# Second layer of a four-layer block: convolution steps split up, z in a buffer of its own, scans and gates on other slots

## The chip, the cores and the metric

One NeuronCore of a Trainium2 chip runs the whole program. The metric is the device time of one execution in microseconds (us), the median of three runs. The engines are TensorE (PE; PEld is its weight load), VectorE (DVE), ScalarE (ACT), GpSimd (POOL) and SyncE (SP), which issues most of the DMAs.

## The reference, cut to what matters

Four layers work on an activation of 256 rows by 2048 columns, in float32. Each layer is: RMS norm, one wide input projection, mixers, a gate, an output projection. The change touches the second one (`odd_layer`):

```python
proj = rmsnorm(x, norm_g) @ w_in
xc, zc, qd, kd, vd, zd, a_pre, b_pre = split_cols(proj, OD_SIZES)
xconv = causal_dwconv(xc, conv_c_w) + conv_c_b              # 4 taps
yc = rg_lru(xconv, gate_w, gate_b, lam) * silu(zc)          # a scan along the 256 rows
qkv = silu(causal_dwconv(concat([qd, kd, vd]), conv_d_w))   # 4 taps
q, k, v = split(qkv, 3); q = l2norm(q); k = l2norm(k)
od = gated_delta_chunkwise(q, k, v, beta, g)
yd = rmsnorm(od, onorm_g) * silu(zd)
y = concat([yc, yd]) @ w_out
```

The kernel does the delta rule over two blocks of 128 rows for each head. The inverse of the unit triangular matrix is made from 16x16 blocks on DVE and then by doubling on PE (levels 4, 5 and 6).

## The kernel before, in words

**Pieces.** All weights come as 626 pieces of at most 128x1024 in float32. ACT copies a piece into a rounded high part (WH, L1062, the function `split`), DVE subtracts for the low part (WL, L1427), and PE multiplies three products of high and low parts (L711 to L713 where rows are the output's partitions, L735 to L737 where features are). Eight raw buffers (L629 loads them), six WH and eight WL buffers are used in turn. During piece p, ACT and DVE split piece p+5.

**Jobs.** Eight pieces (four for some) make a job of 512 output columns, which ends in an evacuation of the accumulator ACC by the engines of its kind (`evacuate`, a function on each engine). Layer 1 (the second one, counted from 0) has these jobs, with their pieces: qd0 177 to 184, kd0 to 192, ab 193, vd0 to 201, qd1 to 209, kd1 to 217, vd1 to 225, xc0 to 233, xc1 to 241, zd0 to 249, zd1 to 257, zc0 to 265, zc1 to 273, and the four output jobs to 305.

**The plan.** Everything but the projections is a step, put by hand on a slot (a piece's number; in layer 1 as `b1 + n` with b1 = 177) by `plan1`. Each engine walks through the slots in order: at slot p it does its split of piece p+5 (PE its products of piece p), its evacuation if a job ends there, and then its part of the steps of that slot in the order in which they were put. So a slot is a place in five queues, and no queue overtakes. Steps that need a PSUM bank on PE get one of four banks (PM) in turn; `bank()` makes PE wait until the last reader of that bank is done.

**Convolution.** CONV lists eight jobs c = 0 to 7 (qd0, kd0, vd0, qd1, kd1, vd1, xc0, xc1), each with two halves i. ACT copies ACC into a ring in S[AA] (L1107) and POOL multiplies by the row norms (L1950). The step `conv` of a half then is: on ACT the last tap for two groups of 128 features (L1237), on DVE six instructions for the other taps (L1669), and for c < 6 on ACT two silu (L1243) that wait for them. Both parts stand on slot L+1 (half 0) and L+3 (half 1), L being the job's last piece.

**After the convolution.** `norm_sq` squares q and k on ACT (L1268); `norm_sum` sums them on PE with one-column matmuls (L917); `delta_a`, `delta_k`, `delta_q` make the matrices; `tri` is the 16x16 inverse (DVE L1765 to L1790, mostly short instructions on few elements; ACT L1299 to L1309); `level_x` is PE L960, then ACT L1319; `level_y` is PE L974 and L977, then DVE L1797 and L1801; `gate_delta` is DVE L1838.

**The recurrence.** `scan` for each of eight groups is three DVE instructions (L1843, L1845, L1847). The z of this branch is evacuated by DVE (job kind "zc", L1455) into S[AA], over the decays that the scans have read, and so waits for those scans. ACT takes its silu (`gate_c`, L1355), POOL multiplies (L2020), and `split_c` makes the high part (ACT L1361) and the low part (DVE L1854) for the output product. The other half of the output's input is turned on PE by `ty` (L891) and split by ACT (L1228) and DVE (L1656).

Of the kernel before, what the change touches and what calls it, by code (L numbers as in the profile page):

```python
# [10 lines left out]
ALU = mybir.AluOpType  # L11
# [141 lines left out]
def program(nc, I, out):  # L153
    ctx = ExitStack()
    with ctx:
# [20 lines left out]
        WH = [sb(f"WH{i}", 1024, F32R) for i in range(NHL)]  # L176
        SC = sb("SC", 4096)
        C = sb("C", CW)
        S5 = sb("S5", 2048)
        S6 = sb("S6", 2048)  # L180
        S0 = sb("S0", 2048)
# [257 lines left out]
        def plan1():  # L439
            b1 = F(1, "qd", 0)  # L440
            put(b1 + 18, "decays1", 0, 1)
            put(b1 + 19, "decays2", 0)
            put(b1 + 23, "decays3", 0, 1)
            for c in range(8):
                put(L(1, *CONV[c]) + 1, "conv", (c, 0))
                put(L(1, *CONV[c]) + 3, "conv", (c, 1))
            for half, at in ((0, (21, 24, 35, 37)), (1, (45, 48, 57, 59))):
                put(b1 + at[0], "norm_sq", half)
                for i in range(2):
                        put(b1 + at[1] + i, "norm_sum", (half, i), 1)  # L450
                for i in range(4):
                    put(b1 + at[2 + i // 2], "turn_v", 4 * half + i, 1)
            for half, diag, delta, tri, level, solve, gate in (
                    (0, (24, 25), (26, 28, 30, 32, 34), (36, 37, 38, 39, 40, 42, 44, 45, 46, 47), (50, 52, 54, 56, 57, 59),
                     (61, 62, 63, 64, 65), (85, 87, 89)),
                    (1, (65, 66), (67, 69, 71, 72, 73), tuple(range(74, 84)), (86, 88, 90, 92, 94, 96), (98, 100, 102, 103, 104),
                     (105, 105, 107))):
                for i in range(2):
                    put(b1 + diag[i], "diag", (half, i))
                for i in range(5):  # L460
                    if i:
                        put(b1 + delta[i], "delta_k", 4 * half + i - 1, 1)
                        put(b1 + delta[i], "delta_q", 4 * half + i - 1, 1)
                    if i < 4:
                        put(b1 + delta[i], "delta_a", 4 * half + i, 1)
                for i in range(10):
                    put(b1 + tri[i], "tri", (half, i))
                for i in range(3):
                    put(b1 + level[2 * i], "level_x", (half, 4 + i), 2)
                    put(b1 + level[2 * i + 1], "level_y", (half, 4 + i), 4)  # L470
                for i in range(4):
                    for j in range(4):
                        put(b1 + solve[i], f"solve{i + 1}", 4 * half + j, 1)
                put(b1 + solve[4], "onorm", half)
                for i in range(2):
                    put(b1 + gate[i], "gate_delta", 2 * half + i)
                    put(b1 + gate[2], "ty", (1, 4 + 2 * half + i), 1)
            put(b1 + 68, "gate_w")
            for n in range(8):
                put(b1 + 74 + n // 2, "gate_lru", n, 1)  # L480
                put(b1 + 78 + n // 2, "decay_lru", n)
                put(b1 + 82 + n // 4, "root_lru", n)
                put(b1 + (84, 85, 86, 87, 90, 92, 94, 95)[n], "scan", n)
            for b in range(2):
                for i in range(2):
                    put(L(1, "zc", b) + 1 + i, "gate_c", (b, i))
                    put(L(1, "zc", b) + 2 + i, "split_c", (b, i))
            out_plan(1)

        def plan2(layer):  # L490
# [552 lines left out]
        def scalar(e):  # L1043
# [185 lines left out]
                else:  # L1229
                    e.activation(YH8[q // 4][:, n:n + 2, :], turned, ACT.Copy).then_inc(s_yh)  # L1230

            def conv(item, _):
                c, i = item
                e.wait_ge(s_cx, 2 * c + i + 1)
                for n, dst, w, src in conv_parts(c, i):
                    if c < 6:
                        e.activation(dst, src, ACT.Copy, scale=w[:, 3:4]).then_inc(s_cw)  # L1237
                    else:
                        e.activation(dst, src, ACT.Identity, scale=w[:, 3:4], bias=vec("cb", n, n + 1)).then_inc(s_cw)
                if c < 6:  # L1240
                    for g, (n, dst, w, src) in enumerate(conv_parts(c, i)):
                        e.wait_ge(s_tap, 12 * c + 6 * i + 5 + g)
                        e.activation(dst, dst, ACT.Silu).then_inc(s_silu)  # L1243

            def decays1(_, b):
                e.wait_ge(s_dt, 1)
# [102 lines left out]

            def gate_c(item, _):  # L1350
                b, i = item
                n = 4 * b + 2 * i
                z = S[AA][:, 256 * n:256 * n + 512]
                e.wait_ge(s_evD, at_D(1, "zc", b) - 1 + i)
                e.activation(z, z, ACT.Silu).then_inc(s_zs)  # L1355

# [10 lines left out]
            def subln(part, _):  # L1367
                if part == 0:
# [1 line left out]
                    e.activation(ss, ss, ACT.Sqrt, bias=vec("eps"), scale=1.0 / 256).then_inc(s_sln)  # L1370

            steps = {"warm": warm, "xt": xt, "squares": squares, "root": root, "rms_a": rms_a, "gates1": gates1, "decay": decay, "pT": pT,
                     "norm_qk": norm_qk, "qkT": qkT, "scores": scores, "mix1": mix1, "pv": pv, "ty": ty, "conv": conv, "decays1": decays1,
                     "decays2": decays2, "norm_sq": norm_sq, "norm_sum": norm_sum, "turn_v": turn_v, "delta_a": delta_a, "tri": tri, "level_x": level_x,
                     "solve4": solve4, "onorm": onorm, "gate_lru": gate_lru, "decay_lru": decay_lru, "root_lru": root_lru,
                     "gate_c": gate_c, "split_c": split_c, "lambda": lambdas, "subln": subln}
# [36 lines left out]
        def vector(e):  # L1413
# [15 lines left out]
            def evacuate(j, p):  # L1429
# [8 lines left out]
                elif J.kind == "few":  # L1438
                    e.wait_ge(s_mm, p + 1)
                    e.tensor_copy(S[5 if J.name == "gif" else XC][0:2 * J.n, 0:256], acc[0][0:2 * J.n, 0:256]).then_inc(s_evD)  # L1440
                elif J.kind == "copy":
                    dst = tok({"vb": 2, "va": 5, "v0": 2, "v1": 5}[J.name])[:, 1, c]
                    e.wait_ge(s_mm, p + 1)
                    e.tensor_scalar(dst, acc[1], rstd[:, 1:2], None, ALU.mult).then_inc(s_evD)
                elif J.kind == "qk":
                    dst = tok(3 if J.name == "qa" else 4)
                    e.wait_ge(s_mm, p + 1)
                    for t in range(2):
                        e.tensor_scalar(dst[:, t, c], acc[t], rstd[:, t:t + 1], None, ALU.mult).then_inc(s_evD)
                elif J.kind == "zc":  # L1450
                    e.wait_ge(s_mm, p + 1)
                    for i in range(2):
                        n = 4 * J.b + 2 * i
                        e.wait_ge(s_ls, 3 * (n + 1) + 3)
                        e.tensor_tensor(two(S[AA][:, 256 * n:256 * n + 512]), two(acc[i]), row2, ALU.mult).then_inc(s_evD)  # L1455
                elif J.kind == "add":
                    e.wait_ge(s_mm, p + 1)
                    for t in range(2):
                        e.tensor_tensor(X3[:, t, c], acc[t], X3[:, t, c], ALU.add).then_inc(s_evD)
                elif J.kind == "rope":  # L1460
                    r = ROPE.index(j)
                    s = int(J.name[1]) * 3 + (J.name[0] == "k")
                    cos, sin = (con(x).unsqueeze(1).broadcast_to([128, 2, 256]) for x in ("cos", "sin"))
                    lo, hi = slice(0, 64), slice(64, 128)
                    dst, t2 = feat(s)[:, 2 * J.b:2 * J.b + 2, :], two(S6[:, 512 * (r % 2):512 * (r % 2) + 512])
                    e.wait_ge(s_mm, p + 1)
                    e.tensor_reduce(dst, halves_of(j), AX, ALU.add).then_inc(s_evD)
                    e.wait_ge(s_row, J.layer + 1)
                    if r > 1:
                        e.wait_ge(s_rot, r - 1)  # L1470
                    e.wait_ge(s_evD, D_AT[j] - 3)
                    for x, y in ((lo, hi), (hi, lo)):
                        e.tensor_tensor(t2[x], dst[y], sin[y], ALU.mult).then_inc(s_evD)
                    e.wait_ge(s_evD, D_AT[j] - 1)
                    e.tensor_tensor(dst, dst, cos, ALU.mult).then_inc(s_evD)  # L1475
# [181 lines left out]
                else:  # L1657
                    e.tensor_tensor(YL8[q // 4][:, n:n + 2, :], turned, hi, ALU.subtract).then_inc(s_yl)

            def conv(item, _):  # L1660
                c, i = item
                done = 12 * c + 6 * i
                e.wait_ge(s_cw, 4 * c + 2 * i + 2)
# [206 lines left out]
            def subln(part, _):  # L1870
# [6 lines left out]
                for h in (2 * part, 2 * part + 1):  # L1877
                    for t in range(2):
# [3 lines left out]
            steps = {"warm": warm, "xt": xt, "rms_a": rms_a, "rms_b": rms_b, "gates1": gates1, "gates2": gates2, "decay_row": decay_row,  # L1882
                     "decay": decay, "mscores": mscores, "norm_qk": norm_qk, "scale_k": scale_k, "scores": scores, "mix1": mix1,
                     "mix2": mix2, "pT": pT, "pv": pv,
                     "finish": finish, "ty": ty, "conv": conv,
                     "decays1": decays1, "decays2": decays2, "decays3": decays3, "norm_sum": norm_sum,
                     "delta_a": delta_a, "delta_k": delta_k, "delta_q": delta_q, "tri": tri, "level_y": level_y,
                     "solve1": solve1, "solve2": solve2, "solve3": solve3, "solve4": solve4, "onorm": onorm, "gate_delta": gate_delta,
# [38 lines left out]
        def gpsimd(e):  # L1927
# [86 lines left out]

            def gate_c(item, _):
                b, i = item
                n = 4 * b + 2 * i
                y = Y3[:, b, 512 * i:512 * i + 512]
                e.wait_ge(s_zs, 2 * b + i + 1)
                e.tensor_tensor(y, y, S[AA][:, 256 * n:256 * n + 512], ALU.mult).then_inc(s_zg)  # L2020

            def load_mask(_, b):
                e.wait_ge(s_mm, F(2, "v0", 0) + 1)
# [95 lines left out]
```

## Time and profile before

| | us |
|---|---|
| median of 3 runs | 1930.18 (1930.12 to 1930.44) |
| the profiled execution | 1932.59 |
| its span | 1930.8 |
| PE busy in it | 1915.4 (99%) |
| DVE busy | 1203.2 (62%) |
| ACT busy | 1017.4 (53%) |
| POOL busy | 165.2 (9%) |
| mean granted TensorE clock | 0.995 |

The span is from the first to the last instruction of the program. The profiled execution's own time has a little more around it (1.8 us). Matmuls overlap, so a busy PE can still have idle cycles; what ends a wait of PE is read from the waits and from the timeline, and the granted clock from the windows.

### The profile page before, as it was taken

The numbers are of one execution on the slowest core, as the hardware profiler recorded it, in microseconds if no ns is written. First come the engines' busy times: TensorE is split into PE (matmuls) and PEld (weight loads), VectorE is DVE, ScalarE is ACT, GpSimd is POOL, SyncE is SP. The second block draws the span as 40 slices with busy tenths as digits, with TensorE's granted clock in tenths as the row PEclk, the third lists the DMA queues.
The fourth block names the chain that finished last, engine by engine and source line by source line (L and its number), as shares of the span: only waits on it lengthen the run. The fifth ranks groups of instructions, "written<-read, shape, count | busy, mean of one in ns | idle before, by whom it ended". The sixth has DMA issues, their size and how long they took to land.

```text
span 1930.8 us, 27225 instructions
## 1 busy us (share of the span) xinstructions
PE 1915.4 (99%) x10884; PEld 1671.6 (87%) x10884; DVE 1203.2 (62%) x1672; ACT 1017.4 (53%) x1583; POOL 165.2 (9%) x142
## 2 busy tenths in 40 slices
PE   9999999999999999999999999999999999999998
PEld 8988888888899999898888888888888888888886
DVE  6455554555566777677656888645555788754553
ACT  7345445664557665764543345556554334445644
POOL 0000000110002101100001211000000121100110
PEclk9999999999999999999999999999999999999999
DMA  9555455555554434434555555554555555455453
GB/s 337 173 184 176 162 188 189 167 164 190 180 174 159 159 125 148 156 130 155 183 195 189 191 176 169 179 181 163 174 180 190 187 188 173 163 186 174 156 203 132
DMA packets 95037, 340.32 MB, mean 176 GB/s; under 512 B 10704, under 2 KB 11472, under 8 KB 94784
## 3 DMA queue, kind: packets, MB, share of 16 engines
q1 hardware_dynamic: 93392, 333.76, 52.2%
q0 software_dynamic: 944, 3.61, 0.6%
q8 instruction: 87, 1.43, 0.3%
q10 hardware_dynamic: 576, 1.21, 0.2%
q14 instruction: 38, 0.31, 0.1%
HBM read 336.44 MB, written 2.10 MB: 175 GB/s over the span
## 4 chain that ended last, share of the span: by engine, by line
PE 93%; DVE 3%; ACT 3%; issue 1%; ACTq 0%
PE ACC L711 18%; PE ACC L713 18%; PE ACC L712 18%; PE ACC L719 6%; PE ACC L716 6%; PE ACC L735 4%; PE ACC L736 4%; PE ACC L737 4%; PE ACC L718 3%; PE ACC L717 3%; DVE WL L1427 1%; ACT WH L1062 1%; PE PM L838 1%; PE PM L891 1%; DVE S L1669 1%
## 5 line engine op out<-in xcount | busy, mean ns | idle before, releaser
L1427 DVE TENSOR_TENSOR WL<-RAW,WH 128x1024 fp32r<-128x1024 f32 (+1 forms) x624 | 793.6, 1288 | 559.6 <-ACT WH L1062 558.7
L1062 ACT ACTIVATE WH<-RAW 128x1024 fp32r<-128x1024 f32 (+1 forms) x626 | 649.7, 1052 | 512.2 <-PE ACC L713 285.7
L711 PE MATMUL ACC<-WH,XHL 128*128 128x512 f32 x1024 | 407.1, 398 | 0.0
L713 PE MATMUL ACC<-WH,XHL 128*128 128x512 f32 x1024 | 399.0, 390 | 0.0
L712 PE MATMUL ACC<-WL,XHL 128*128 128x512 f32 x1024 | 398.7, 389 | 0.0
L735 PE MATMUL ACC<-XHL,WH 128*128 128x256 f32 x872 | 252.1, 289 | 0.0
L736 PE MATMUL ACC<-XHL,WH 128*128 128x256 f32 x872 | 248.5, 285 | 0.0
L737 PE MATMUL ACC<-XHL,WL 128*128 128x256 f32 x872 | 248.4, 285 | 0.0
L713 PEld LDWEIGHTS ACC<-WH,XHL 128*128 128x128 f32 x1024 | 192.2, 188 | 40.7
L712 PEld LDWEIGHTS ACC<-WL,XHL 128*128 128x128 f32 x1024 | 192.4, 188 | 39.1
L711 PEld LDWEIGHTS ACC<-WH,XHL 128*128 128x128 f32 x1024 | 192.3, 188 | 38.6
L716 PE MATMUL ACC<-XHL,WH 128*128 128x512 f32 x512 | 205.3, 401 | 0.0
L719 PE MATMUL ACC<-XHL,WH 128*128 128x512 f32 x512 | 202.5, 396 | 0.0
L735 PEld LDWEIGHTS ACC<-XHL,WH 128*128 128x128 f32 x872 | 169.3, 194 | 0.6
L736 PEld LDWEIGHTS ACC<-XHL,WH 128*128 128x128 f32 x872 | 169.3, 194 | 0.2
L737 PEld LDWEIGHTS ACC<-XHL,WL 128*128 128x128 f32 x872 | 169.1, 194 | 0.0
L718 PE MATMUL ACC<-XHL,WL 128*128 128x256 f32 x512 | 142.5, 278 | 0.0
L717 PE MATMUL ACC<-XHL,WL 128*128 128x256 f32 x512 | 142.1, 277 | 0.0
L718 PEld LDWEIGHTS ACC<-XHL,WL 128*128 128x128 f32 x512 | 96.1, 188 | 23.4
L717 PEld LDWEIGHTS ACC<-XHL,WL 128*128 128x128 f32 x512 | 96.3, 188 | 21.8
L1955 POOL TENSOR_TENSOR S<-S 128x512 f32<-128x512 f32 x32 | 66.9, 2092 | 479.6 <-DVE S L1475 479.6
L711 PE MATMUL ACC<-WH,YHB 128*128 128x512 f32 x256 | 101.0, 394 | 0.0
(365 smaller groups left out, 2433.4 us busy)
## 6 DMA issues: line engine op xcount, KB each, us to landing
RAW<-in_w SPq DMA_DIRECT2D x621, 512.0 KB, 3.3
X<-in_x SPq DMA_DIRECT2D x4, 512.0 KB, 9.8
RAW<-in_w SPq DMA_DIRECT2D x6, 256.0 KB, 4.4
Y<-in_xT SPq DMA_DIRECT2D x2, 512.0 KB, 12.2
S<-in_bias POOLq DMA_DIRECT2D x8, 128.0 KB, 2.4
S<-in_od_gate_w POOLq DMA_DIRECT2D x1, 1024.0 KB, 6.9
S<-in_final_norm POOLq DMA_DIRECT2D x1, 1024.0 KB, 8.5
out<-Y SPq DMA_DIRECT2D x2, 512.0 KB, 2.6
```

The lines of the kernel that those rows point to most:

```text
L711: e.matmul(o, th, hi[:, kk, :], start=f, stop=False)
L712: e.matmul(o, th, lo[:, kk, :], start=False, stop=False)
L713: m = e.matmul(o, tl, hi[:, kk, :], start=False, stop=l)
L716: e.matmul(acc[0], wh0, XHL3[:, kt, :], start=f, stop=False, skip_group_check=True)
L717: e.matmul(acc[0][:, 0:256], wl0, xh, start=False, stop=l, skip_group_check=True)
L718: e.matmul(acc[1][:, 0:256], wl1, xh, start=f, stop=False, skip_group_check=True)
L719: m = e.matmul(acc[1], wh1, XHL3[:, kt, :], start=False, stop=l, skip_group_check=True)
L735: e.matmul(o, wh, xh, start=f and g % 2 == 0, stop=False, skip_group_check=True)
L736: e.matmul(o, wh, xl, start=False, stop=False, skip_group_check=True)
L737: m = e.matmul(o, wl, xh, start=False, stop=l, skip_group_check=True)
L1062: e.activation(hi, src, ACT.Copy).then_inc(s_hi)
L1427: e.tensor_tensor(lo, src, hi.bitcast(F32), ALU.subtract).then_inc(s_lo)
```

## The change

The step `conv` becomes three: `copied` (ACT, last tap), `taps` (DVE) and `silu` (ACT). Their slots after a job's last piece are 1 and 2, 2 and 4, and 3 and 5 for the halves 0 and 1. `norm_sq` of half 1 and its `norm_sum` go one slot later. The z branch gets a buffer ZC of 128x1024 that both of its jobs use in turn: zc0 is evacuated with no wait for scans, zc1 waits until POOL has read zc0's (`s_zg`, 2). The wait for the scans is now in POOL's `gate_c`. Of the scans 1, 2, 3, 4, 5 and 6 move from b1+85, 86, 87, 90, 92, 94 to b1+86, 88, 90, 91, 92, 93; the gate of delta half 0 moves from b1+85 and 87 to b1+94 and 97, and its `ty` from b1+89 to b1+101; `gate_c` and `split_c` of zc0 move from slots 266 to 268 to b1+92 to b1+94 (269 to 271).

```diff
+        ZC = sb("ZC", 1024)
...
             for c in range(8):
-                put(L(1, *CONV[c]) + 1, "conv", (c, 0))
-                put(L(1, *CONV[c]) + 3, "conv", (c, 1))
-            for half, at in ((0, (21, 24, 35, 37)), (1, (45, 48, 57, 59))):
+                for i in range(2):
+                    put(L(1, *CONV[c]) + 1 + i, "copied", (c, i))
+                    put(L(1, *CONV[c]) + 2 + 2 * i, "taps", (c, i))
+                    if c < 6:
+                        put(L(1, *CONV[c]) + 3 + 2 * i, "silu", (c, i))
+            for half, at in ((0, (21, 24, 35, 37)), (1, (46, 49, 57, 59))):
...
-                     (61, 62, 63, 64, 65), (85, 87, 89)),
+                     (61, 62, 63, 64, 65), (94, 97, 101)),
...
-                put(b1 + (84, 85, 86, 87, 90, 92, 94, 95)[n], "scan", n)
+                put(b1 + (84, 86, 88, 90, 91, 92, 93, 95)[n], "scan", n)
             for b in range(2):
                 for i in range(2):
-                    put(L(1, "zc", b) + 1 + i, "gate_c", (b, i))
-                    put(L(1, "zc", b) + 2 + i, "split_c", (b, i))
+                    put((b1 + 92, L(1, "zc", 1) + 1)[b] + i, "gate_c", (b, i))
+                    put((b1 + 93, L(1, "zc", 1) + 2)[b] + i, "split_c", (b, i))
...
-            def conv(item, _):
+            def copied(item, _):
...
-                if c < 6:
-                    for g, (n, dst, w, src) in enumerate(conv_parts(c, i)):
-                        e.wait_ge(s_tap, 12 * c + 6 * i + 5 + g)
-                        e.activation(dst, dst, ACT.Silu).then_inc(s_silu)
+
+            def silu(item, _):
+                c, i = item
+                for g, (n, dst, w, src) in enumerate(conv_parts(c, i)):
+                    e.wait_ge(s_tap, 12 * c + 6 * i + 5 + g)
+                    e.activation(dst, dst, ACT.Silu).then_inc(s_silu)
...
                 b, i = item
-                n = 4 * b + 2 * i
-                z = S[AA][:, 256 * n:256 * n + 512]
+                z = ZC[:, 512 * i:512 * i + 512]
...
                 elif J.kind == "zc":
                     e.wait_ge(s_mm, p + 1)
+                    if J.b:
+                        e.wait_ge(s_zg, 2)
                     for i in range(2):
-                        n = 4 * J.b + 2 * i
-                        e.wait_ge(s_ls, 3 * (n + 1) + 3)
-                        e.tensor_tensor(two(S[AA][:, 256 * n:256 * n + 512]), two(acc[i]), row2, ALU.mult).then_inc(s_evD)
+                        e.tensor_tensor(two(ZC[:, 512 * i:512 * i + 512]), two(acc[i]), row2, ALU.mult).then_inc(s_evD)
...
-            def conv(item, _):
+            def taps(item, _):
...
                 y = Y3[:, b, 512 * i:512 * i + 512]
+                e.wait_ge(s_ls, 12 * b + 6 * i + 6)
                 e.wait_ge(s_zs, 2 * b + i + 1)
-                e.tensor_tensor(y, y, S[AA][:, 256 * n:256 * n + 512], ALU.mult).then_inc(s_zg)
+                e.tensor_tensor(y, y, ZC[:, 512 * i:512 * i + 512], ALU.mult).then_inc(s_zg)
```

## Rows read from the trace of the kernel before

**Rows 1.** The page, busy time of each engine and share of the span.
```profile
PE 1915.4 (99%) x10884; PEld 1671.6 (87%) x10884; DVE 1203.2 (62%) x1672; ACT 1017.4 (53%) x1583; POOL 165.2 (9%) x142
```

**Rows 2.** Waits of PE, whole run: us in total, times, longest.
```profile
PE PM L891 <- DVE SC L1797: 3.8, 1, 3.8
PE PM L917 <- ACT S L1268: 2.3, 1, 2.3
...
PE PM L960 <- issue: 0.2, 1, 0.2
```

**Rows 3.** Timeline of PE: start, duration, engine, line [idle before <- releaser].
```profile
692.76 2.89 PE L917 MATMUL PM<-C,S 128*128 128x1 f32 x16 [2.31 <-ACT S L1268]
700.60 1.84 PE L917 MATMUL PM<-C,S 128*128 128x1 f32 x16
...
854.85 1.94 PE L891 MATMUL PM<-C,Y 128*128 128x128 f32 x8 [3.83 <-DVE SC L1797]
```

**Rows 4.** Windows of PE: stretch, us, busy (matmuls), granted clock, DMA share, GB/s.
```profile
611.50:618.30 6.80, 6.80 (x59) 1.00 0.41 141
...
693.54:700.37 6.83, 6.83 (x34) 0.50 0.01 2
...
854.85:860.79 5.94, 5.94 (x28) 0.50 0.00 0
```

**Rows 5.** Windows: PE, PEld, DVE, ACT, POOL busy, clock, DMA.
```profile
661.33:700.37 39.04, 36.73 (x282) 36.53 (x281) 33.53 (x94) 22.66 (x45) 3.52 (x2) 0.91 0.46 149
```

**Rows 6.** Waits of ACT, whole run.
```profile
ACT S L1243 <- DVE S L1669: 31.3, 12, 6.8
```

**Rows 7.** Timeline of ACT, end of the convolutions.
```profile
672.08 0.91 ACT L1237 ACTIVATE S<-S,VC 128x256 f32<-128x256 f32 x2 [1.01 <-POOL S L1950]
679.81 0.81 ACT L1243 ACTIVATE S<-S 128x256 f32<-128x256 f32 x2 [6.83 <-DVE S L1669]
...
687.55 0.81 ACT L1243 ACTIVATE S<-S 128x256 f32<-128x256 f32 x2 [4.23 <-DVE S L1669]
...
690.16 2.54 ACT L1268 ACTIVATE S<-S 128x256 f32<-128x256 f32 x8
```

**Rows 8.** Timeline of DVE, the same stretch.
```profile
671.08 1.03 DVE L1777 TENSOR_TENSOR SC<-SC 128x40 f32<-128x40 f32 x1
...
677.73 2.45 DVE L1669 SCALAR_TENSOR_TENSOR S<-S,VC 128x255 f32<-128x255 f32 x6
681.61 1.22 DVE L1427 TENSOR_TENSOR WL<-RAW,WH 128x1024 fp32r<-128x1024 f32 x1 [1.43 <-ACT WH L1062]
```

**Rows 9.** Timeline of DVE before PE's second wait.
```profile
839.04 1.23 DVE L1427 TENSOR_TENSOR WL<-RAW,WH 128x1024 fp32r<-128x1024 f32 x1 [2.36 <-ACT WH L1062]
840.19 0.42 DVE L1843 SCALAR_TENSOR_TENSOR Y<-S,Y 128x256 f32<-128x256 f32 x1
...
841.71 1.20 DVE L1427 TENSOR_TENSOR WL<-RAW,WH 128x1024 fp32r<-128x1024 f32 x1
842.82 1.13 DVE L1838 SCALAR_TENSOR_TENSOR Y<-Y,SM,S 128x128 f32<-128x128 f32 x4
...
852.83 1.28 DVE L1455 TENSOR_TENSOR S<-ACC,C 128x512 f32<-128x512 f32 x2
854.03 0.68 DVE L1797 TENSOR_TENSOR SC<-SC,PM 128x512 f32<-128x512 f32 x1
...
856.42 1.22 DVE L1427 TENSOR_TENSOR WL<-RAW,WH 128x1024 fp32r<-128x1024 f32 x1
```

**Rows 10.** Timelines of ACT and POOL: the z branch and a table load.
```profile
619.09 1.28 ACT L1277 ACT_TABLE_LOAD   x1
...
863.61 0.62 ACT L1355 ACTIVATE S<-S 128x512 f32<-128x512 f32 x1
...
883.45 2.51 POOL L2020 TENSOR_TENSOR Y<-Y,S 128x512 f32<-128x512 f32 x1 [17.86 <-ACT S L1355]
887.99 1.28 POOL L2020 TENSOR_TENSOR Y<-Y,S 128x512 f32<-128x512 f32 x1 [2.03 <-ACT S L1355]
```

More of the change, by code:

```diff
@@ L1372, in scalar @@
             steps = {"warm": warm, "xt": xt, "squares": squares, "root": root, "rms_a": rms_a, "gates1": gates1, "decay": decay, "pT": pT,
-                     "norm_qk": norm_qk, "qkT": qkT, "scores": scores, "mix1": mix1, "pv": pv, "ty": ty, "conv": conv, "decays1": decays1,
+                     "norm_qk": norm_qk, "qkT": qkT, "scores": scores, "mix1": mix1, "pv": pv, "ty": ty, "copied": copied, "silu": silu, "decays1": decays1,
                      "decays2": decays2, "norm_sq": norm_sq, "norm_sum": norm_sum, "turn_v": turn_v, "delta_a": delta_a, "tri": tri, "level_x": level_x,
@@ L1884, in vector @@
                      "mix2": mix2, "pT": pT, "pv": pv,
-                     "finish": finish, "ty": ty, "conv": conv,
+                     "finish": finish, "ty": ty, "taps": taps,
                      "decays1": decays1, "decays2": decays2, "decays3": decays3, "norm_sum": norm_sum,
@@ L2016, in gate_c @@
                 b, i = item
-                n = 4 * b + 2 * i
                 y = Y3[:, b, 512 * i:512 * i + 512]
+                e.wait_ge(s_ls, 12 * b + 6 * i + 6)
                 e.wait_ge(s_zs, 2 * b + i + 1)
-                e.tensor_tensor(y, y, S[AA][:, 256 * n:256 * n + 512], ALU.mult).then_inc(s_zg)
+                e.tensor_tensor(y, y, ZC[:, 512 * i:512 * i + 512], ALU.mult).then_inc(s_zg)
             def load_mask(_, b):
```

## The prediction

> **What bounds the kernel now.** I read the page's busy times first: PE is busy for 99% of the span, DVE 62%, ACT 53% [rows 1]. PE has no spare work to shed here, and the change takes no matmul away, so it can only win what PE loses in waits and in clock. The waits of PE come next [rows 2]: one of 3.8 us on DVE L1797, one of 2.3 us on ACT L1268, 1.5 us at the start, 0.2 us at L960. The timeline says where the first two stand [rows 3]: 2.31 us ahead of 692.76, at the norm sums of half 1, and 3.83 us ahead of 854.85, at `ty` of delta half 0. Both are in the layer that the change touches. The windows give what follows each [rows 4]: from 693.54 to 700.37 and from 854.85 to 860.79 the granted clock is 0.50, that is 1.2 GHz, against 1.00 (2.4 GHz) elsewhere, and PE gets 34 and 28 matmuls through where an ordinary stretch of 6.80 us holds 59. PE had been idle just before both. The trace shows no other long wait of PE in this layer.
>
> The losses are thus: wait one 2.31. Low clock one: 34 matmuls at the ordinary 6.80 / 59 = 0.115 us are 3.9 us of work in 6.83, so 2.9 lost; half of the stretch would be 3.4; I take 3.1. Wait two 3.83. Low clock two: 28 x 0.115 = 3.2 in 5.94, so 2.7 lost, by the half 3.0; I take 2.9. Together 2.31 + 3.1 + 3.83 + 2.9 = 12.1 us (11.7 to 12.5).
>
> **Part 1, copies, taps and silu apart.** What made ACT late for wait one is in its timeline [rows 7]: before each pair of silu it stood idle for the taps, 6.83 us before 679.81 and 4.23 us before 687.55, and then did the splits and `norm_sq` (2.54 us from 690.16). Over the whole run such waits are 31.3 us in 12 cases, one for each silu pair [rows 6]. DVE meanwhile came to these taps only at 677.73, because the short instructions of `tri` stand ahead of them in its queue; and right after the taps it waited itself, 1.43 us for ACT's split at 681.61, which stood behind the silu [rows 8]. Each waits for the other in turn, twice a job.
>
> In the new plan the silu of a half is a slot behind its taps, and the taps of half 0 are a slot behind their copies. The instructions are the same. What changes is the order of ACT's functions, and with it the table loads, 1.28 us each [rows 10]: silu (1,1) comes behind `decays2`, one load more; the two norm sums of each half no longer have a silu between them, which saves two each; the silu of job 2 stand between the delta steps, two more at most. By the order of the plan it is 15 loads before and 14 after from slot 195 to 230; I take 0 (from 1.3 us saved to 1.3 us more on ACT), and it is hidden: in 661.33:700.37 ACT is busy 22.66 of 39.04 us [rows 5].
>
> Can DVE hold the pace? In that stretch it is busy 33.53 of 39.04 us [rows 5]. PE's undisturbed time for the same slots, 39.04 - 2.31 - 3.1 = 33.6 us, is as much as DVE has to do. DVE falls back by at most a few us over these slots (the taps that move in from slot 210 to 211 and 212 to 213 are 2.45 us more), but its slack is five pieces for a split, 5 x 24 matmuls x 0.115 = 14 us, and for wait one the new chain is taps at slot 221, silu at 222, `norm_sq` at 223, PE at the end of 226. That is over five slots, some 14 us, for 2.45 + 0.81 + 2.54 us and three splits of some 1.0 us: it is ready 5 us early even if DVE is a slot late. Next in line is `level_x` at slot 227, which needs the end of `tri` (slot 224). PE reached it at 700.60 + 1.84 + a piece of 2.9, 705.3 [rows 3], and will be there 5.4 earlier, at about 700. `tri` ended with the window of rows 5, at 700.4, in which DVE was idle for 39.04 - 33.53 = 5.5 us; without most of that it ends before 698. So wait one goes whole, its cost on the path is 0, and with its cover gone a late `tri` would cost 0 to 2 us. `norm_sq` and `norm_sum` one slot later have nothing behind them but `level_x`; PE's 16 one-column matmuls are 1.84 us at full clock wherever they stand [rows 3]. Gain 2.31 + 3.1 = 5.4.
>
> **Part 2, scans, gates and z.** At wait two PE stood in `ty` for a bank that DVE L1797 had not read. DVE's queue up to it [rows 9]: it starts the split of slot 261 at 839.04, having waited for ACT, and then without a pause does, through slot 265, five splits, four scans (each from 840.19 to 841.71, 1.5 us), two steps of `gate_delta` (each 1.1 to 1.15 us, 842.82), the evacuation of zc0 from 852.83 (1.2 us) and `level_y` from 854.03 to 856.42. The new plan has scans 0 and 1 ahead of `level_y` instead of four, and neither `gate_delta`: 2 x 1.5 + 2 x 1.1 = 5.2 us less. The evacuation starts at about 847.6 and `level_y` runs from 848.9 to 851.2. PE had finished the matmuls of `level_y` one piece ahead of its wait, at 854.85 - 3.83 - 24 x 0.12 = 848.1, so the z evacuation no longer has anything late ahead of it either. And `ty` is gone from slot 266. PE's next use of these banks is `level_x` at the end of piece 267, at 848.1 + 2 x 2.9 = 853.9. DVE is 2.7 us early. Wait two goes whole: gain 3.83 + 2.9 = 6.7.
>
> What is late next? From slot 266 to 273 DVE now has 8 splits (9.2), scans 3 to 7 (7.5; scan 2 runs at the end of 265), `level_y` 5 and 6 (some 3.3 by the row of 854.03 to 856.42 for the first), one `gate_delta` (1.1), two `split_c` (some 1.4, bounded by the 0.68 of L1797's equal shape), the evacuation of zc1 (1.2): 23.7 us against eight pieces of PE, 8 x 2.9 = 23.2, plus its own steps (three `level_x` and `level_y`, some 4 us). DVE starts 5 us behind and ends no further behind; `level_y` 5 needs it at the end of slot 269 and gives PE two pieces. I take 0, with 0 to 2 us as bound. `ty` at slot 278 is four pieces (11 us) ahead of the output piece that reads it. The new waits: POOL's `gate_c` on the scans has only POOL's own `gate_c` behind it, which had idle times of 17.86 and 2.03 us ahead of it [rows 10]. DVE's new wait for `s_zg` 2 at the end of slot 273 holds `level_y` 6 behind it, and PE's solves wait for that; it is met when ACT's two silu (0.62 each, one load of 1.28) and POOL's two products (1.28 to 2.51 each) are done, 5.1 to 7.5 us after slot 269 begins, and four slots are 11.6 us. ZC itself has no cost: the same shapes are written and read.
>
> **A rule against it.** While POOL worked in this stretch, one DVE instruction on 128x40 took 1.03 us [rows 8], and POOL's product took 2.51 us in one place and 1.28 in another [rows 10]. The Trainium skill, "SBUF — State Buffer", section "SBUF: two separate sides", has VectorE (with two inputs in SBUF) and GpSimd take turns at a shared pair of ports, each held for a whole instruction; the trace agrees. By that rule the two products of zc0, which move to slots 269 and 270, where DVE is full, would hold DVE for up to 2 x 1.28 = 2.6 us more, and the sum for slots 266 to 273 would stand at 26.3 us instead of 23.7, against PE's 27. That is no wait of PE yet; it takes the margin of rival (b).
>
> **The rivals.**
> (a) The waits go, one low clock stays: norm sum (1,1) and `level_x` 4 now meet at slot 227, 1.84 us of one-column matmuls and then 16 small ones, with no wide piece between. For it: the first drop came at such a sum. Against: it had 2.31 us of idle ahead, which go. Time: 1930.2 - 12.1 + 3.1 = 1921.2.
> (b) One wait comes back or is replaced: DVE is close to PE's pace in both places. Wait two shrinks to 2 us, and the clock falls all the same: 12.1 - 2 - 3 = 7.1 gained, 1923.1. Wait one alone stays: 5.4 less, 1923.5. For it: DVE's margin of 2.7 us at slot 267 rests on one sum.
> (c) ACT and DVE are late from something else than each other, so that no wait shrinks: 1930.2. For it: only that DVE is 86% busy in its stretch. Against: the idle times in rows 7 and 8.
> (d) Slower: DVE stands at slot 273 for `s_zg`. Decides: the handing on from ACT to POOL starts over 4 us after slot 269. If all of the 7.5 us is exposed and the clock then falls (3 us), and if the same lateness hits `ty` at 278 (two ACT copies and two DVE subtractions of 128x512, some 2.8 us) with its own fall of 3 us, PE loses 16.3 us; 1930.2 - 12.1 + 16.3 = 1934.4. Against: PE's slack there is several pieces.
>
> **How the numbers follow.** The profiled execution took 1932.6, 2.4 above the median; it would take 1932.6 - 12.1 = 1920.5, and the median of such runs 1930.2 - 12.1 = 1918.1. Spacing of matmuls around each wait is 0.15 us more than the idle time that the trace tells, so I put the forecast at 1917.9. Chances: both waits and both drops gone 0.74; (a) 0.08; (b) 0.10; (c) 0.04; (d) 0.04. The likeliest's own range is 1916.5 to 1920 (losses counted by half the clock, up to 2 us of new waits). The whole range goes to 1923.5, to take in (a) and most of (b). What a measurement can tell from no change is 0.2%, 3.9 us: below 1926.3 is faster. (a) and (b) are both that, so faster 0.91, same 0.05, slower 0.04.
>
> **What would show it.** Right: no wait of PE over 0.3 us in the layer besides L960's; the clock at 1.00 from 600 to 1000 us; the waits of ACT L1243 on DVE L1669 down from 31.3 us to under 5; DVE's L1797 of level 4 done before PE is at slot 267's end. Wrong: a PE wait at L960 or L974 after slot 227 or 266 (b), a drop of the clock with no wait ahead (a), DVE L1455 waiting for POOL L2020 (d).

## The result, and the profile after

The changed kernel took 1919.62 us (median of four runs, 1919.2 to 1920.32), the kernel before 1930.31 (1930.12 to 1931.5): ratio 0.994, 95% interval 0.9928 to 0.9952. It is faster by 10.7 us; the forecast was 1917.9. In the later measurements the kernel before stood at 1930.95 to 1931.8, since its executions spread from 1930.0 to 1932.7.

The page and PE's waits of the changed kernel answer [rows 1, 2]. Its lines are numbered 4 to 6 higher (L921 is the norm sum, L964 `level_x`, L978 and L981 `level_y`, L1249 silu, L1274 `norm_sq`, L1432 the split, L1674 taps). Both long waits are gone, and the clock is at 1.00 where it had fallen.

```profile
span 1917.5 us, 27227 instructions
PE 1908.2 (100%) x10884; PEld 1665.5 (87%) x10884; DVE 1203.8 (63%) x1672; ACT 1016.9 (53%) x1582; POOL 165.0 (9%) x142
```

```profile
PE PM L769 <- DVE S L1483: 1.5, 1, 1.5
PE PM L964 <- issue: 0.2, 1, 0.2
```

Windows of PE in the changed kernel (stretch, us, busy, matmuls, clock, DMA), which answer [rows 4]:

```profile
611.50:618.30 6.80, 6.80 (x60) 1.00 0.29 94
690.27:697.30 7.03, 7.03 (x63) 1.00 0.44 150
600.00:1000.00 400.00, 399.79 (x2832) 1.00 0.49 161
```

Three marks on PE say where the time came from. The first is the first norm sum, the second `level_x` 4 of half 1 with its wait of 0.2 us, the third the end of the span. PE's timeline of the kernel before, then of the changed one:

```profile
609.83 1.84 PE L917 MATMUL PM<-C,S 128*128 128x1 f32 x16
...
836.80 0.57 PE L960 MATMUL PM<-SC,S 128*128 128x128 f32 x3 [0.20 <-issue]
```

```profile
608.86 1.84 PE L921 MATMUL PM<-C,S 128*128 128x1 f32 x16
...
830.19 2.02 PE L964 MATMUL PM<-SC,S 128*128 128x128 f32 x16 [0.21 <-issue]
```

Up to the first mark 0.97 us came off, which is not the change's doing: PE is ahead by that much after 8 us of the span, long before layer 1, and by no more at the first mark. Between the marks it is 226.97 against 221.33, 5.64 us, the first part of the change. From the second mark to the end it is 1930.8 - 836.80 = 1094.00 against 1917.5 - 830.19 = 1087.31, 6.69 us, the second part.

ACT's and PE's timelines round the old first wait, in the changed kernel, answer [rows 3, 7]:

```profile
676.57 0.81 ACT L1249 ACTIVATE S<-S 128x256 f32<-128x256 f32 x2 [3.20 <-DVE S L1674]
677.29 1.99 ACT L1066 ACTIVATE WH<-RAW 128x1024 fp32r<-128x1024 f32 x2
682.78 0.81 ACT L1249 ACTIVATE S<-S 128x256 f32<-128x256 f32 x2 [3.51 <-DVE S L1674]
...
684.46 2.55 ACT L1274 ACTIVATE S<-S 128x256 f32<-128x256 f32 x8
...
691.22 1.73 ACT L1315 ACTIVATE SC<-SC 32x256 f32<-32x256 f32 x4 [3.27 <-DVE SC L1789]
```

```profile
692.20 1.84 PE L921 MATMUL PM<-C,S 128*128 128x1 f32 x16
696.86 1.84 PE L921 MATMUL PM<-C,S 128*128 128x1 f32 x16
698.57 2.03 PE L964 MATMUL PM<-SC,S 128*128 128x128 f32 x16
```

`norm_sq` now ends at 687.0, 5.2 us ahead of PE, and `tri`'s last copies at 692.95, 5.6 us ahead of `level_x`. Where two waits of ACT had been 6.83 and 4.23 us, they are 3.20 and 3.51, and nothing of PE's hangs on them.

DVE's queue ahead of the old second wait, changed kernel, answers [rows 9]:

```profile
832.43 1.23 DVE L1432 TENSOR_TENSOR WL<-RAW,WH 128x1024 fp32r<-128x1024 f32 x1 [2.36 <-ACT WH L1066]
...
841.11 1.28 DVE L1460 TENSOR_TENSOR ZC<-ACC,C 128x512 f32<-128x512 f32 x2
842.31 0.68 DVE L1802 TENSOR_TENSOR SC<-SC,PM 128x512 f32<-128x512 f32 x1
...
844.10 0.68 DVE L1806 TENSOR_TENSOR SC<-SC,PM 128x512 f32<-128x512 f32 x1
```

From its start to the instruction behind `level_y` (844.70 here) the queue takes 12.3 us instead of 17.4, 5.1 us less (forecast 5.2). The last read of a bank ends at 844.78, and PE takes the banks up at 847.22, 2.4 us later (forecast 2.7).

### The profile page after: what moved, and what is told of

It is laid out like the page before. It is cut to its first block, busy times and chain, and to the rows that moved or that the text cites. A ratio compares the mean times of both kernels' runs of the same rounds, so it can differ in the third digit from the quotient of the medians.

```text
span 1917.5 us, 27227 instructions
## 1 busy us (share of the span) xinstructions
PE 1908.2 (100%) x10884; PEld 1665.5 (87%) x10884; DVE 1203.8 (63%) x1672; ACT 1016.9 (53%) x1582; POOL 165.0 (9%) x142
## 4 chain that ended last, share of the span: by engine, by line
PE 100%; ACT 0%; DVE 0%; issue 0%
PE ACC L715 18%; PE ACC L717 18%; PE ACC L716 18%; PE ACC L723 6%; PE ACC L720 6%; PE ACC L739 6%; PE ACC L740 5%; PE ACC L741 5%; PE ACC L722 3%; PE ACC L721 3%; PE PM L842 1%; PE PM L857 1%; PE PM L895 1%; PE PM L879 1%; PE PM L880 1%; PE PM L878 1%
## 5 line engine op out<-in xcount | busy, mean ns | idle before, releaser
L1432 DVE TENSOR_TENSOR WL<-RAW,WH 128x1024 fp32r<-128x1024 f32 (+1 forms) x624 | 794.6, 1289 | 545.7 <-ACT WH L1066 544.3
L739 PEld LDWEIGHTS ACC<-XHL,WH 128*128 128x128 f32 x872 | 167.2, 192 | 0.6
L740 PEld LDWEIGHTS ACC<-XHL,WH 128*128 128x128 f32 x872 | 167.2, 192 | 0.2
```

The costliest lines, as they stand in the source:

```text
L739: e.matmul(o, wh, xh, start=f and g % 2 == 0, stop=False, skip_group_check=True)
L740: e.matmul(o, wh, xl, start=False, stop=False, skip_group_check=True)
L1432: e.tensor_tensor(lo, src, hi.bitcast(F32), ALU.subtract).then_inc(s_lo)
```

## The experiments

Twelve runs in three groups of four, in the order b_again, conv_only, scans_only, filled; norm_later, norm_early, gate_only, z_scans_only; silu_apart, silu_with_taps, conv_gate, level_later. Each group ran on a chip of its own, with its own runs of the kernel before (medians 1931.83, 1931.76 and 1930.95). Ratios are to those, with 95% intervals. With the result's 1930.31 these differ by up to 1.5 us, so medians of different groups can't be compared more closely than that; the marks at the end of this section do better.

**b_again.** The kernel before, unchanged.

> The kernel before, once more. The median of the changed kernel is 10.7 us under this one's, but its profiled execution 12.9 us under. Theory: what the two low-clock stretches cost differs between executions, since they begin at another place each time; then the executions of this kernel differ in span and in granted clock, with spans from 1928 to 1931 us, and the waits of 2.3 and 3.8 us are in its trace again. Rival: recording costs this kernel some 2 us and the changed one nothing; then all executions have a span of about 1930.8 and a clock of 0.995.

1931.82 us, ratio 0.9998 (0.9989 to 1.0007). The profiled execution took 1930.12 and had a span of 1928.2 and a clock of 0.997, so executions do differ. Windows of PE in it:

```profile
693.88:697.29 3.41, 3.41 (x19) 0.50 0.00 0
...
854.31:857.72 3.41, 3.41 (x19) 0.50 0.00 0
```

The low clock lasts 3.41 us after each wait, not 6.83 and 6. By the same marks: 608.30 to the first (1.5 us less than in the other execution), 226.99 to the second (the same), 1092.91 to the end (1.1 less). The 1.5 us at the start all arise in the first 8 us (PE, kernel before, then b_again):

```profile
4.00:7.00 3.00, 3.00 (x5) 1.00 1.04 353
```

```profile
4.00:7.00 3.00, 3.00 (x11) 1.00 1.02 345
```

So half of the first stretch of low clock went, 1.6 us, and nothing came of it. PE's timeline shows why: it waits again, 1.05 us at `level_y`, and once more within the 32 matmuls of `level_x` 5 (1.01 us instead of 0.70 in the first execution).

```profile
691.25 1.95 PE L917 MATMUL PM<-C,S 128*128 128x1 f32 x16 [2.32 <-ACT S L1268]
...
710.90 0.46 PE L974 MATMUL PM<-SC 128*128 128x128 f32 x2 [1.05 <-issue]
...
720.39 1.01 PE L960 MATMUL PM<-SC 32*32 32x32 f32 x32
```

The trace names no engine for the wait of 1.05 us ("issue"). The timelines of ACT and DVE do. Kernel before, then b_again:

```profile
711.73 1.08 ACT L1319 ACTIVATE SC<-PM 128x512 f32<-128x512 f32 x2
...
721.74 0.68 DVE L1801 TENSOR_TENSOR SC<-SC,PM 128x512 f32<-128x512 f32 x1
```

```profile
710.21 1.08 ACT L1319 ACTIVATE SC<-PM 128x512 f32<-128x512 f32 x2
...
720.23 0.68 DVE L1801 TENSOR_TENSOR SC<-SC,PM 128x512 f32<-128x512 f32 x1
```

Counted from the first mark, ACT begins its copies of `level_x` 4 at 101.9 us in both, and DVE ends `level_y` 4 at 112.6 us in both, however fast PE is. `level_y` begins 0.7 us after the copies do, here as in scans_only, filled, norm_later and silu_with_taps, where PE stands waiting. In the first execution PE's own delays brought it there 0.4 us later than that, so it had no wait.

**conv_only.** The changed kernel with z, scans and gates as before.

> Only the first part of the change (copied, taps and silu apart, norm_sq and norm_sum of half 1 a slot later); scans, gates and z as before. Theory, each part removes its own wait and the low clock behind it: PE's wait of 2.3 us on ACT L1268 and the drop at 693 are gone, the wait of 3.8 us at ty stays with its drop; 4.4 to 5.9 us faster, 1924.4 to 1925.9. Rival, ACT and DVE that run ahead in slots 200 to 225 also help later: the second wait shrinks as well, over 8 us faster.

1924.8 us, ratio 0.9963 (0.9951 to 0.9976). The time is in the expected range, the gain is not: 7.0 us, from a median of 1931.83 with more long executions in it than the 1930.3 from which the range was made. PE's first wait is gone, the second is left:

```profile
PE PM L894 <- DVE SC L1802: 3.8, 1, 3.8
```

**scans_only.** The kernel before with ZC, the scans and the gates of the change.

> Only the second part (z in ZC, scans and gates moved), the convolution step as before. Theory: the wait of 3.8 us and its drop go, the first wait of 2.3 us and its drop stay; 5.8 to 7.3 us faster, 1923.0 to 1924.5. Rival, the first wait's low clock alone also costs later waits: less than 5 us faster.

1925.49 us, ratio 0.9968 (0.9955 to 0.998), 6.3 us faster. Here the gain is in the expected range and the time is above it, for the same reason. The first wait is left (2.3 us), with the wait of 1.05 us at `level_y` that b_again had too. Each part removes its own wait and leaves the other's; in that both theories held.

**filled.** On scans_only:

```diff
                 half, part = item
+                o = bank(b)
+                if item == (1, 0):
+                    for _ in range(3):
+                        e.matmul(o, ident, C[:, 0:512], start=True, stop=True, skip_group_check=True)
                 e.wait_ge(s_nsq, half + 1)
-                o = bank(b)
```

> As scans_only, and PE does three matmuls of 128x512 into the bank that it is about to use while it waits for norm_sq of half 1 (their result is overwritten). Theory, the clock falls because PE is idle: the wait's place is filled, the clock stays at 1.00, and the run is 2.5 to 3.5 us faster than scans_only, with the norm sums starting no earlier. Rival, the one-column matmuls of the norm sums make the clock fall: it falls again and the time is that of scans_only.

Neither came out. 1926.73 us, ratio 0.9974 (0.9963 to 0.9984), 1.2 us slower than scans_only in the same group. The clock did stay up at the norm sums. Timeline of PE (five of the six records that the three wide matmuls leave), then of ACT, then windows of PE:

```profile
689.56 2.31 PE L915 MATMUL PM<-C 128*128 128x512 f32 x5
691.70 1.85 PE L921 MATMUL PM<-C,S 128*128 128x1 f32 x16
...
711.28 0.46 PE L978 MATMUL PM<-SC 128*128 128x128 f32 x2 [2.56 <-ACT SC L1323]
```

```profile
709.63 1.05 ACT L1066 ACTIVATE WH<-RAW 128x1024 fp32r<-128x1024 f32 x1
710.58 1.08 ACT L1323 ACTIVATE SC<-PM 128x512 f32<-128x512 f32 x2
```

```profile
693.88:697.30 3.42, 3.42 (x33) 1.00 0.00 0
711.65:715.07 3.42, 3.42 (x18) 0.50 0.00 0
```

PE came 2.56 us early to `level_y`, waited for ACT's copies of `level_x`, and the clock fell there instead. In scans_only `level_y` began at 710.95, here at 711.28; from the first mark that is 102.6 us in both. ACT sets that time: it is late from the convolution on, and whatever PE saves ahead of it is waited off.

**norm_later.** scans_only with `norm_sq` and `norm_sum` of half 1 on b1 + 46 and 49, as in the change.

> scans_only with one edit more: norm_sq and norm_sum of half 1 a slot later, as in the full change, but the convolution step in one piece. Theory, it is the lateness of ACT and DVE that PE pays for and not the place: the wait at L917 shrinks from 2.3 us to under 0.7, and one of 2 to 3 us comes at level_y (L974), with low clock behind it; the time stays within 1.2 us of scans_only's 1925.5. Rival, the slot was one too early and the split of the step does little: the time comes near the full change, 1919.5 to 1921.

1926.38 us, ratio 0.9973 (0.9963 to 0.9984), as the theory has it:

```profile
PE PM L975 <- ACT SC L1320: 2.9, 1, 2.9
```

The low clock behind that wait is there too (712.12 to 715.53). But the trace has a second one that nobody expected, earlier, after the norm sums and with no wait of PE over 0.2 us ahead of it. PE's timeline and window:

```profile
692.78 1.95 PE L918 MATMUL PM<-C,S 128*128 128x1 f32 x16
```

```profile
695.06:698.47 3.41, 3.41 (x19) 0.50 0.08 32
```

So an idle PE is not the only thing ahead of which the clock falls. The changed kernel runs the same norm sums without a wait and without a fall. Why it fell here stays open.

**norm_early.** The changed kernel with them on b1 + 45 and 48.

> The full change with norm_sq and norm_sum of half 1 back on their old slots. Theory, splitting the step leaves enough margin: no wait of PE at L921, same time as the changed kernel, 1919.2 to 1920.3. Rival, the slot carries part of the gain: a wait of 0.5 us or more at the norm sums, 1920.5 to 1924.

1919.48 us, ratio 0.9936 (0.9924 to 0.9949), no wait there. So the slot of the norm is worth nothing, with or without the split of the step (between the two marks 221.33 us here and in the changed kernel).

**silu_apart.** The changed kernel with

```diff
-                    put(L(1, *CONV[c]) + 1 + i, "copied", (c, i))
-                    put(L(1, *CONV[c]) + 2 + 2 * i, "taps", (c, i))
+                    put(L(1, *CONV[c]) + 1 + 2 * i, "copied", (c, i))
+                    put(L(1, *CONV[c]) + 1 + 2 * i, "taps", (c, i))
```

> The changed kernel with copied and taps back together on slots L+1 and L+3, and only silu apart, two slots on (L+3, L+5). Theory, what counts is that ACT doesn't stand for the taps with splits queued behind it: same as the changed kernel, 1919.2 to 1920.4, no wait of PE at the norm sums or level_y. Rival, the slot between copies and taps counts too (DVE waits for the copies): 0.5 us or more slower.

1919.8 us, ratio 0.9941 (0.9928 to 0.9953). The waits of ACT's silu for the taps are 1.3 us in two cases here, against 9.3 us in five in the changed kernel:

```profile
ACT S L1249 <- DVE S L1674: 1.3, 2, 0.9
```

**silu_with_taps.** The changed kernel with silu on the slots of its taps:

```diff
-                        put(L(1, *CONV[c]) + 3 + 2 * i, "silu", (c, i))
+                        put(L(1, *CONV[c]) + 2 + 2 * i, "silu", (c, i))
```

> The changed kernel with silu on the slots of its taps (L+2, L+4), so that only the copies are apart. Theory, ACT and DVE wait for each other as before: ACT's waits on the taps add up to over 20 us again, PE waits 1 us or more at the norm sums or at level_y of half 0, 1921 to 1925. Rival, the later slots alone are enough: 1919.2 to 1920.4.

1927.0 us, ratio 0.9977 (0.9968 to 0.9986): 7.4 us over the changed kernel, which was measured in another group, and worse than expected. ACT's waits are back, and PE has a wait of 4.2 us at `level_y`:

```profile
ACT S L1249 <- DVE S L1674: 34.0, 12, 7.0
```

```profile
PE PM L978 <- ACT SC L1325: 4.2, 1, 4.2
```

With silu_apart: silu a slot or two behind its taps is the whole of the first part.

**gate_only.** The kernel before with

```diff
-                     (61, 62, 63, 64, 65), (85, 87, 89)),
+                     (61, 62, 63, 64, 65), (94, 97, 101)),
```

> The kernel before with only the gate of delta half 0 and its ty moved (to b1+94, 97 and 101); scans, z and its waits as before. Theory, by DVE's queue: level_y is done 2.1 us sooner, at 854.3 instead of 856.4, and PE's next use of the banks is level_x at 853.9, so the wait of 3.8 us is down to under 0.5 and the drop goes; as scans_only, 1925.0 to 1926.2. Rival, the z evacuation behind four scans is what counts: a wait of 1 us or more at level_x, 1926.5 to 1930.

1925.77 us, ratio 0.9967 (0.9954 to 0.9979). The wait of 3.8 us is 0.2:

```profile
PE PM L960 <- DVE SC L1801: 0.2, 1, 0.2
```

**z_scans_only.** scans_only with that line as before.

> scans_only with the gate of delta half 0 and its ty back on b1+85, 87 and 89: z in ZC and the scans spread, no more. Theory: DVE has two scans less ahead of level_y, 3.1 us, so the wait at ty is 0.5 to 1.2 us instead of 3.8 and too short for the clock to fall; 1925.5 to 1927. Rival, ty in its old slot keeps both the wait over 2 us and the drop: 1928 to 1930.

1926.85 us, ratio 0.9974 (0.9964 to 0.9985). The wait at `ty` is 0.8 us and the clock stays up behind it:

```profile
PE PM L892 <- DVE SC L1797: 0.8, 1, 0.8
```

So each half of the second part does nearly all of its work: 3.1 us of scans or 2.1 us of gates (and the place of `ty`) out of DVE's way.

**conv_gate.** conv_only with gate_only's line: no ZC, scans as before.

> The convolution part and the moved gate of delta half 0 with its ty; scans and z as before. Theory, by conv_only and gate_only, which removed one wait each, the gains add, and the buffer ZC and the spread scans give nothing but margin: 1919.3 to 1920.6, with a wait of about 0.2 us at level_x 5 as in gate_only. Rival, with PE earlier the wait at level_x grows and the clock falls: 1922 or more.

1920.33 us (1919.42 to 1920.76), ratio 0.9942 (0.9928 to 0.9955), with a wait of 0.2 us at `level_x` 5. Its runs overlap with those of the changed kernel. Whether ZC and the spread scans are worth some tenths can't be told from these; the marks below say 0.4 us.

**level_later.** The changed kernel with `level_x` 4 of half 1 on b1 + 87.

> The changed kernel with level_x 4 of half 1 on b1+87 instead of 86. It is the place of PE's last wait in the layer, 0.2 us. Theory: that wait goes, level_y a slot behind still finds ACT done; 0.2 to 0.3 us less span, 1919.2 to 1919.4 as median, at the edge of what can be told. Rival: PE waits 0.5 us or more at L978 for ACT's copies, 1920 to 1921.

1919.97 us (1918.91 to 1920.2), ratio 0.994 (0.9928 to 0.9953). PE's last wait in the layer is gone from the trace and no other came, but the time, above the 1919.2 to 1919.4 expected, can't be told from the changed kernel's. No version tried is clearly faster than that one.

**All kernels by the two marks.** The start of an execution differs by up to 1.6 us whatever the kernel, and this is in every median. The marks leave it out. For each profiled execution, in us:

| kernel | low clock between the marks | first mark to second | second mark to the end |
|---|---|---|---|
| before | 6.83, norm sums | 226.97 | 1094.0 |
| b_again | 3.41, norm sums | 226.99 | 1092.9 |
| scans_only | 3.41, norm sums | 227.02 | 1087.3 |
| gate_only | 6.83, norm sums | 227.05 | 1087.7 |
| z_scans_only | 6.83, norm sums | 227.02 | 1088.4 |
| filled | 3.41, `level_y` | 228.32 | 1087.3 |
| norm_later | 3.41, norm sums, and 3.41, `level_y` | 228.24 | 1087.3 |
| silu_with_taps | 6.83, `level_y` | 228.56 | 1087.3 |
| conv_only | none | 221.33 | 1093.0 |
| conv_gate | none | 221.34 | 1087.7 |
| silu_apart, norm_early, the changed kernel | none | 221.33 | 1087.3 |

The first part of the change is worth 5.6 to 5.7 us in the column from mark to mark, with the second part and without it. The second part shows in the last column: 6.7 us against the execution with the long low clock, 5.6 against that with the short one, and of this 0.4 for ZC and the spread scans beside the moved gate. In level_later the second mark itself is a piece later; from the first mark to the end it takes 1308.2 us against 1308.6, so 0.4 us less, which the start hides.

## Why the prediction was right, and where not

**The mechanism** was right in both parts. The edits remove PE's two waits and the low clock behind each, add no wait, and the rest is hidden. silu_apart and silu_with_taps show for the first that it is silu on the slot of its taps, where ACT and DVE wait for each other; gate_only and z_scans_only show for the second that it is DVE's queue ahead of `level_y`.

**The sum** was right for the execution from which it was made: 12.1 us forecast, 0.3 more for the spacing; 5.64 between the marks (forecast 5.4) and 6.69 behind them (6.7). The table loads, taken as 0, came out at one fewer, as the plan had it: the page counts 1583 instructions of ACT before and 1582 after.

**What was mis-sized** is the step from that execution to the median. The forecast put the 2.4 us by which the profiled execution is above the median outside of the sum, as if both kernels had them, and took the whole 12.1 from 1930.2. By b_again these are 1.5 us ahead of the first mark and 1.1 us of low clock after wait two, which the change removes. So low clock two, 2.9 us in the sum and 2.9 in the profiled execution (6.69 - 3.83), is 1.8 in the short kind of execution (5.60 - 3.83). Such an execution had only 5.66 + 5.60 = 11.3 us to win behind the first mark, and 1930.2 - 11.3 = 1918.9. The changed kernel's profiled execution reached the first mark 0.6 us later than b_again's (608.86 against 608.30), which gives 1919.5; measured is 1919.6. Against the median of 1931.8 in the second group norm_early, which has the changed kernel's time, gains 12.3.

**Low clock one as a term** (3.1 us; 5.64 - 2.31 = 3.3 measured) was in part a wrong account that gave the right sum. I took it as a loss on top of the wait. b_again and scans_only have half of it and are no faster between the marks; filled has none of it there and is slower. What stands behind it is the lateness of ACT and DVE: PE can't begin `level_y` 4 before 102.6 us after the first mark, nor go past the middle of `level_x` 5 before 112.6. In the changed kernel it is at the first at 97.3 and at the middle of the second at 107.0, so 5.3 and 5.6 us earlier. PE pays this in wait, low clock and further waits in whatever mix. That wait one and its low clock came to just this much in the profiled execution, so that PE had no second wait there, was luck.

**The waits of ACT's silu** were forecast under 5 us and are 9.3, five waits of up to 3.5 us, the two shown above among them. That DVE comes to these taps late, behind `tri`, is argued from the plan. They are hidden; silu_apart has 1.3 and the same time.

**The rival (a)**, a drop of the clock where norm sums and `level_x` meet, did not come: PE's rows of the changed kernel have them in a row from 696.86 to 700.6, and the clock is 1.00 from 600 to 1000 us. The reason given against it, that the idle time ahead goes, is not enough by norm_later, where the clock fell soon after one-column matmuls with no wait ahead. (b), (c) and (d) did not come either. For (d): POOL's second product, which DVE waits for, ended at 858.4, and DVE reached the evacuation of zc1 at 869.2.

**The rule against it**, DVE and POOL in turn at two products, stood in the prediction as up to 2.6 us more on DVE. The changed kernel's timelines of DVE and POOL at slots 269 and 270:

```profile
857.28 1.40 DVE L1850 TENSOR_TENSOR S<-S,Y 128x256 f32<-128x256 f32 x1
```

```profile
854.22 1.29 POOL L2025 TENSOR_TENSOR Y<-Y,ZC 128x512 f32<-128x512 f32 x1 [47.95 <-ACT ZC L1360]
856.83 1.58 POOL L2025 TENSOR_TENSOR Y<-Y,ZC 128x512 f32<-128x512 f32 x1 [1.33 <-ACT ZC L1360]
```

One DVE instruction with two inputs took 1.40 us instead of 0.42 while POOL worked; the first product met none. The cost was 1.0 us and hidden.

## What to carry to other kernels

Where two engines work through a common plan in order, don't put a consumer on the slot of its producer: the consumer's queue stands still, the producer then waits for what is queued behind the consumer, and here the engine that bounds the kernel paid for it with 5.6 us. Removing that lateness was worth what PE had lost by it; hiding the place where it was paid, by a later slot (norm_later) or by filler (filled), only moved the bill and made it 1.2 to 1.3 us longer. Before a sum is carried from a profile to a median, look at two executions: a clock loss in it may be of another length in the runs. And to compare variants that differ by less than the spread of the runs, count from a mark behind the start.

## What was not expected of the hardware

The granted clock fell after every wait of PE of 2.3 us or more in layer 1 (2.3 to 2.4 us in five executions, then 2.6, 2.9, 3.8 and 4.2), and stayed at 0.50 for 3.41 us in one execution of the kernel before and for 6.83 us in the other; the other kernels show one or the other length. It did not fall after waits of 0.8 and 1.05 us. It did not fall either when PE did three wide matmuls in a wait of 2.3 us, nor over 3.7 us of one-column and small matmuls without a wait (from 696.86 in the changed kernel). But it fell once, in norm_later, at 695.06, with no wait over 0.2 us ahead, so the idle time is not the whole of it. The start of the same kernel took 1.5 us longer in one execution than in another, all of it in the first 8 us.
